# Gate and up products of an expert block in two 256-column halves, their inner rows formed and turned by halves

## The reference

```
for e in range(16):
    he = silu(t @ w_exp_gate[e]) * (t @ w_exp_up[e])          # 2048 -> 512
    out = out + gates[:, e:e+1] * (he @ w_exp_down[e])        # 512 -> 2048
```

## Time and profile before

| | |
|---|---|
| median of 3 runs | 1512.7 us (1511.94 to 1514.83) |
| profiled execution | 1513.4 us, its span 1511.6 us |
| mean granted TensorE clock | 0.973 |
| TensorE matmuls busy | 1381.8 us, 91% |
| weight loads / VectorE / ScalarE / GpSimd busy | 42% / 50% / 16% / 5% |
| DMA | 422.25 MB, mean 279 GB/s |
| expert stage: L976, first gate and up matmul | 992.5 us |
| expert stage: last down matmul ends, L1014 starts | 1483.8 us |

### The profile page before, as it was taken

How to read it: one execution, slowest core, us unless ns; L and a number is a source line. 1 busy time by engine, 2 the same in 40 slices (tenths; PEclk the granted TensorE clock), 3 DMA queues, 4 the chain that set the end, 5 groups by cost and what they waited for, 6 DMA issues and landing times.

```text
span 1511.6 us, 14234 instructions
## 1 busy us (share of the span) xinstructions
PE 1381.8 (91%) x5266; PEld 633.4 (42%) x5266; DVE 753.8 (50%) x1305; ACT 243.3 (16%) x409; POOL 75.5 (5%) x124
## 2 busy tenths in 40 slices
PE   4999999999998799999999999889898987898887
PEld 1435544444554455555544444533333332333332
DVE  1118799987767998989896612620000000000006
ACT  3101421000011111111122001511111111101104
POOL 2002000000010000000001000000000000000001
PEclk9999999999999899999999999989999999999989
DMA  9998656884677733331328634799999999999996
GB/s 356 409 373 261 230 184 227 272 266 147 198 252 267 246 109 105 104 118 64 113 82 311 221 111 167 284 380 426 428 406 414 427 427 427 427 396 426 426 411 274
DMA packets 138130, 422.25 MB, mean 279 GB/s; under 512 B 10230, under 2 KB 76033, under 8 KB 120949
## 3 DMA queue, kind: packets, MB, share of 16 engines
q1 hardware_dynamic: 124452, 375.85, 65.3%
q0 software_dynamic: 7520, 33.36, 6.1%
q10 hardware_dynamic: 6096, 12.20, 2.1%
HBM read 408.01 MB, written 22.58 MB: 285 GB/s over the span
## 4 chain that ended last, share of the span: by engine, by line
PE 68%; DMA 13%; DVE 12%; issue 3%; ACT 2%; SPq 0%; POOL 0%; DVEq 0%; ACTq 0%; POOLq 0%
PE ps L580 19%; PE ps L976 12%; PE ps L577 12%; DMA s_mem<-in_w_exp_gate 8%; PE ps L996 7%; DVE s_mem L1691 4%; DMA s_mem<-in_w_ada 4%; PE ps L497 3%; PE ps L858 3%; DVE s_mem L1895 2%; PE ps L755 1%; DVE s_mem L1866 1%; PE ps L439 1%; PE ps L706 1%; PE ps L454 1%
## 5 line engine op out<-in xcount | busy, mean ns | idle before, releaser
L1691 DVE SCALAR_TENSOR_TENSOR s_mem<-s_mem,s_sT 128x512 f32<-128x512 f32 x480 | 339.3, 748 | 32.9 <-DMA s_mem<-in_w_ada 16.1
L577 PE MATMUL ps<-s_mem 128*128 128x384 f32 x896 | 300.8, 491 | 0.0
L580 PE MATMUL ps<-s_mem 128*128 128x512 f32 x672 | 293.0, 594 | 0.7 <-ACT s_mem L1476 0.7
L976 PE MATMUL ps<-s_mem 128*64 128x512 f32 x1152 | 261.0, 610 | 18.4 <-DMA s_mem<-in_w_exp_gate 17.7
L577 PEld LDWEIGHTS ps<-s_mem 128*128 128x128 f32 x896 | 168.1, 191 | 124.9 <-issue 18.1
L580 PEld LDWEIGHTS ps<-s_mem 128*128 128x128 f32 x672 | 126.3, 190 | 158.3 <-issue 157.1
L976 PEld LDWEIGHTS ps<-s_mem 128*64 128x64 f32 x1152 | 88.0, 141 | 187.6 <-issue 186.7
L2197 DVE TENSOR_TENSOR s_mem<-s_mem,ps 64x512 f32<-64x512 f32 x18 | 12.2, 679 | 299.5 <-ACT s_mem L1568 299.5
L996 PE MATMUL ps<-s_mem 128*64 128x512 f32 x576 | 142.8, 654 | 9.3 <-DVE s_mem L2199 9.3
L996 PEld LDWEIGHTS ps<-s_mem 128*64 128x64 f32 x576 | 43.3, 148 | 95.4 <-issue 83.7
L2204 DVE COPY s_mem<-ps 128x512 f32<-128x512 f32 x18 | 12.4, 691 | 140.8 <-PE ps L996 140.8
(11 more groups left out here) (308 smaller groups left out, 1087.0 us busy)
## 6 DMA issues: line engine op xcount, KB each, us to landing
s_mem<-in_w_ada SPq DMA_DIRECT2D x256, 256.0 KB, 3.2
s_mem<-in_w_exp_gate SPq DMA_DIRECT2D x32, 2048.0 KB, 21.0
s_mem<-in_w_exp_up SPq DMA_DIRECT2D x32, 2048.0 KB, 24.9
s_mem<-in_w_exp_down SPq DMA_DIRECT2D x32, 2048.0 KB, 25.0
s_mem<-in_w_in SPq DMA_DIRECT2D x24, 2048.0 KB, 10.6
s_mem<-in_w_ada SPq DMA_DIRECT2D x16, 2048.0 KB, 16.6
s_mem<-in_w_out SPq DMA_DIRECT2D x8, 2048.0 KB, 9.7
y_slots<-s_mem ACTq DMA_DIRECT2D x34, 256.0 KB, 10.4
```

Of the source, the lines that this page charges most:

```text
L577: m = mm(ps[:, banks[m_], 0:TOK], v[:, k, m_ * P:(m_ + 1) * P], hT[:, kk, :], start=(kk == 0), stop=(kk == KT - 1))
L580: m = mm(ps[:, banks[m_], :], hT[:, kk, m_ * P:(m_ + 1) * P], v[:, k, :], start=(kk == 0), stop=(kk == KT - 1))
L976: m = mm(ps[half, 0, :], hgT[:, kh * 8 + k, :], weights(e, 2 * kh + which)[:, k, :], start=(kh + k == 0), stop=(kh * 8 + k == KT - 1), ski ...
L1691: v.op(ve.scalar_tensor_tensor(out=o, in0=w, scalar=scale, in1=o, op0=ALU.mult, op1=ALU.add), S("piece_used") if last else None)
```

## The change

Gate and up are computed in two halves of 256 columns. The loop over halves (nh) stands inside the loop over the two halves of the contraction (kh), so there are 128 matmuls of 256 columns in place of 64 of 512. A half doesn't take neighbouring columns: a view takes columns with index 0 and 1 modulo 4 for the first, 2 and 3 for the second, so that what the turns took with a step of four now lies contiguous in `he`. The first half stands in bank 0, the second in bank 7. A semaphore `first_half` is raised at the end of the first half. ScalarE and VectorE form `sg`, `he` and `heT` by halves. On TensorE the order after the products is: two turns for the first half (into bank 1), the row turns, a wait for the first turned half, the first of four down steps (4 matmuls each), two turns for the second half (into bank 0), the second step, a wait, the third and fourth. The down matmuls themselves stay as they are. Ahead of the first block TensorE waits until VectorE has read bank 7.

```diff
+        HALF_BANK = (0, 7)
...
             def expert_block(e, b):
-                pe.wait_ge(S("he_ready"), b + 1)
+                pe.wait_ge(S("he_ready"), b * 2 + 1)
                 pe.wait_ge(S("x_turned"), b * 2 + 2)
                 for kh in range(2):
                     for which in range(2):
                         weights_in(e, 2 * kh + which)
-                    for k in range(8):
-                        for which in range(2):
-                            half = slice(BLK * which, BLK * (which + 1))
-                            m = mm(ps[half, 0, :], hgT[:, kh * 8 + k, :], weights(e, 2 * kh + which)[:, k, :],
-                                   start=(kh + k == 0), stop=(kh * 8 + k == KT - 1), skip_group_check=True)
-                            if k == 7:
-                                m.then_inc(S(f"used{2 * kh + which}"), 1)
+                    for nh in range(2):
+                        for k in range(8):
+                            for which in range(2):
+                                half = slice(BLK * which, BLK * (which + 1))
+                                w = weights(e, 2 * kh + which)[:, k, :].rearrange("p (r q) -> p q r", q=4)
+                                out = ps[half, HALF_BANK[nh], 0:DE // 2].rearrange("p (q r) -> p q r", q=2)
+                                m = mm(out, hgT[:, kh * 8 + k, :], w[:, 2 * nh:2 * nh + 2, :], start=(kh + k == 0),
+                                       stop=(kh * 8 + k == KT - 1), skip_group_check=True)
+                                if k == 7 and nh == 1:
+                                    m.then_inc(S(f"used{2 * kh + which}"), 1)
+                                elif k == 7 and kh == 1 and which == 1:
+                                    m.then_inc(S("first_half"), 1)
+                def turn_hidden(h):
+                    pe.wait_ge(S("he_ready"), b * 2 + 2 + h)
+                    pe.nop(nofuse=True)
+                    for q in range(2):
+                        m = tr(ps[:, 1 - h, q * BLK:(q + 1) * BLK], he[:, (2 * h + q) * P:(2 * h + q + 1) * P],
+                               ident[0:BLK, 0:BLK])
+                    m.then_inc(S("he_turns"), 1)
+                def down_step(k):
+                    for n in range(4):
+                        half = slice(BLK * (n % 2), BLK * (n % 2 + 1))
+                        m = mm(ps[half, 4 + n // 2, :], heT[:, k, :], weights(e, 4 + k // 2)[:, k % 2, n * NCOL:(n + 1) * NCOL],
+                               start=(k == 0), stop=(k == 3), skip_group_check=True)
+                    if k % 2 == 1:
+                        m.then_inc(S(f"used{4 + k // 2}"), 1)
+                turn_hidden(0)
                 pe.wait_ge(S("x_gathered"), b * 16 + 16)
                 pe.nop(nofuse=True)
                 turn_rows()
-                pe.wait_ge(S("he_ready"), b + 2)
-                pe.nop(nofuse=True)
-                for q in range(4):
-                    m = tr(ps[:, 1, q * BLK:(q + 1) * BLK], he[:, q:DE:4], ident[0:BLK, 0:BLK])
-                m.then_inc(S("he_turns"), 1)
-                pe.wait_ge(S("he_turned"), b + 2)
+                pe.wait_ge(S("he_turned"), b * 2 + 2)
                 pe.wait_ge(S("y_read_act"), b + 1)
                 pe.wait_ge(S("y_read_dve"), b + 1)
...
+                weights_in(e, 4)
+                down_step(0)
+                turn_hidden(1)
+                down_step(1)
+                pe.wait_ge(S("he_turned"), b * 2 + 3)
+                weights_in(e, 5)
+                down_step(2)
+                down_step(3)
+
+            wait_read(pe, "dve", "index")
...
             def silu(b):
-                act.wait_ge(S("used3"), b + 2)
-                act.wait_ge(S("he_ready"), b + 1)
-                A(sg, ps[BLK:2 * BLK, 0, :], ACT.Silu).then_inc(S("sg_ready"), 1)
+                act.wait_ge(S("he_ready"), b * 2 + 1)
+                for h in range(2):
+                    act.wait_ge(*((S("first_half"), b + 1), (S("used3"), b + 2))[h])
+                    A(sg[:, h * DE // 2:(h + 1) * DE // 2], ps[BLK:2 * BLK, HALF_BANK[h], 0:DE // 2], ACT.Silu
+                      ).then_inc(S("sg_ready"), 1)
...
             def hidden(b):
-                dve.wait_ge(S("used3"), b + 2)
-                dve.wait_ge(S("sg_ready"), b + 1)
-                ve.tensor_tensor(he, sg, ps[0:BLK, 0, :], ALU.mult).then_inc(S("he_ready"), 1)
-                dve.wait_ge(S("he_turns"), b + 1)
-                ve.tensor_copy(heT.rearrange("p k s -> p (k s)"), ps[:, 1, 0:4 * BLK]).then_inc(S("he_turned"), 1)
+                for h in range(2):
+                    cols = slice(h * DE // 2, (h + 1) * DE // 2)
+                    dve.wait_ge(*((S("first_half"), b + 1), (S("used3"), b + 2))[h])
+                    dve.wait_ge(S("sg_ready"), b * 2 + 1 + h)
+                    ve.tensor_tensor(he[:, cols], sg[:, cols], ps[0:BLK, HALF_BANK[h], 0:DE // 2], ALU.mult
+                                     ).then_inc(S("he_ready"), 1)
+                    dve.wait_ge(S("he_turns"), b * 2 + 1 + h)
+                    ve.tensor_copy(heT[:, 2 * h:2 * h + 2, :].rearrange("p k s -> p (k s)"), ps[:, 1 - h, 0:2 * BLK]
+                                   ).then_inc(S("he_turned"), 1)
```

## The result

| | before | after |
|---|---|---|
| median | 1512.3 us (4 runs, 1511.90 to 1514.83) | 1701.4 us (4 runs, 1698.14 to 1702.34) |
| ratio after / before | | 1.123 [1.1211, 1.1249] |
| profiled execution, its span | 1513.4, 1511.6 | 1702.34, 1700.5 |
| mean granted TensorE clock | 0.973 | 0.987 |

The change makes the kernel 12.3% slower. The forecast was 1508.0 us, with a range up to 1513.5. The rival "strided reads at half rate", at 1679 us and a chance of 0.13, is what happened.

A forecast was written before the change was run, and what follows sets the result against it. The weights' arrival at 428 GB/s was taken to bound the expert stage, with TensorE costing 5.5 us in two holes. Closing all but 0.8 us gains 4.7 us, giving 1508.0 us, range 1505.0 to 1513.5.

The forecast's parts named there:

- strided reads at half rate: Gate and up take 27.6 us a block, a block 36.5, so TensorE sets the pace: 1679 us; chance 0.13.
- (b) Stride: Gate and up's moving operand read at every fourth float: priced at nothing; bounds nothing and half rate, 13.8 us a block.
- (a) Halves: Gate and up as 128 matmuls of 256 columns: 0.3 us a block taken, 0.6 at most, nothing at least.
- (c) The stop: TensorE's stop between gate/up and down: 2.0 us for 4.0, with table load, Silu and product off the path.
- (d) Waits and queues: Added waits and changed engine order cost nothing; the first block's bank wait, nothing to 0.3 us, taken as nothing.
- What bounds the kernel: Expert stage: weights' arrival at 428 GB/s, 31.8 us against TensorE's 26.6 a block; TensorE costs 5.5 us in two holes.
- The sum, 4.7 us: Two holes in the expert stage: 5.5 us lost, 0.8 left, the end following, hence 1508.0 us.
- hole: Dip in weight transfer at each expert with two blocks, as slot reloads wait for second block: 3.0 and 2.5 us.

The follow-up runs named there:

- layout alone: Kernel before with only the down matrix loaded as rows k*128 + p (8 KB runs) and `he` turned from contiguous columns: 1515.9 us, ratio 1.0025.
- change without stride: Changed kernel with halves of 256 neighbouring columns and the down matrix loaded as rows k*128 + p in 8 KB runs: 1514.0 us, ratio 1.0005.
- two neighbours: Changed kernel with halves taking columns {0, 1} and {2, 3} of every four, `he` turned in steps of two: 1512.2 us, ratio 0.9985.
- The two cut kernels: Kernel before and version reading two neighbours, each with half of every gate and up piece not loaded from the tenth load on: 1487.6 and 1450.9 us.

## Why the forecast was wrong

One block's gate and up, 64 pairs of 512 columns or 128 matmuls in pairs of 256, by how the moving operand is read. All are pieces of chains at the full granted clock:

| kernel | read | us a block |
|---|---|---|
| before, and layout alone | contiguous | 13.78 |
| change without stride | contiguous, halves | 13.81 |
| stride 8 bytes | 2 of each 16 bytes | 14.55 |
| two neighbours | 2 of each 16 bytes, halves | 14.50 |
| **changed kernel** | 1 of each 16 bytes, halves | 28.87 |
| stride 16 bytes | 1 of each 16 bytes | 28.85 |
| stride 32 bytes | 1 of each 32 bytes | 29.43 |

**(b) Stride: the step that failed**, "I take nothing, since the row has that rate per element with a wider stride". The price is 28.87 - 13.81 = 15.1 us a block, above the upper bound of 13.8. It makes a block 37.7 us, above the 31.8 that the transfers need, so that TensorE sets the pace and every block pays. The forecast had weighed the Trainium skill's rule ("Advanced Engine Details and Errata", SBUF Cachelines: lines of 16 bytes, at least two hits on one to keep the rate) against L915's load and let the load win. The table bears the rule out in the main on the moving side: two hits a line cost 5%, where the rule would have them free, one hit doubles the time, and a wider step adds 2%.

What was wrong was the comparison, not the row. L915's strided load (194 ns) was set against the moving side's pace per column. The like of it is another turn's load, and the trace of before had them, in the list of groups:

```profile
L915 PEld LDWEIGHTS ps<-s_base,s_mem 128*128 128x128 f32 x152 | 18.4, 194 | 16.2 <-issue 16.2
...
L883 PEld LDWEIGHTS ps<-s_base,s_mem 128*128 128x128 f32 x48 | 5.2, 142 | 1.6 <-ACT s_mem L1537 1.4
...
L797 PEld LDWEIGHTS ps<-s_base,s_mem 128*128 128x128 f32 x48 | 5.0, 140 | 6.3 <-ACT s_mem L1476 5.1 <-issue 0.9 <-DVE s_mem L1658 0.3
```

L797 and L883 turn contiguous columns in 140 and 142 ns. The step was in plain sight as 54 ns, and the run with contiguous turns made 140 of the 194. Nor does the stationary side scale to the moving one: 39% there, 109% here. Bounded by half rate the sum was open from 1508 to 1679 us, and the value was taken at one end of it on a row of the other side of the array.

**(a) Halves: right.** 13.81 against 13.78, 0.03 us for the 0.3 taken.

**(c) The stop: right in kind, cheaper.** 1.63 us (1.85 with turns that step by two) for the 2.0. One part didn't go as said: the table load does not come in the last quarter but at the block's start, at 1187.43. Before, it came after the wait for `used3`. In the code the wait that stands directly ahead of the Silu was `he_ready` and is now `first_half` or `used3`; I take it that the load goes ahead of the last wait. That order alone was not tried.

**(d) Waits and queues: right.** No wait for the added semaphores stands in the chain.

**What bounds the kernel: right.** The two cut kernels and the 53.0 and 44.1 us of waiting for weights show it. It is also why a stop that is 2 us shorter in 18 blocks gives 2.3 us in all.

**The sum, 4.7 us: of the right kind, too large.** It belongs to a change that costs no stride; two neighbours to a read is the nearest. The load that opens a hole should be issued 2.5 us before the one ahead lands. Measured are 1135.6 against 1138.2, 2.6 before, so the first hole is closed; and 1331.0 against 1331.7, 0.7 before, so 1.8 us of the second stay, where 0.4 was forecast. That is 3.7 us by the queue, and 2.3 (0.4 to 4.2) by the run times. The second falls short in the stretch from the gate load's landing to the issue: it began with a half block that took 9.06 us after a wait, against 7.47 in the first hole, and took 25.4 us in all where 24.8 were charged.

**The rival's own size.** It took the pairs at exactly half rate (27.6 us) and the stop at 2.0, hence 36.5 us a block and 1679. Measured are 28.87 and 1.63, 37.66 a block. 18 x 1.16 = 21 us of the 22 between 1679 and 1701.

## What to carry to other kernels

Read a moving operand so that at least two neighbouring floats of every 16 bytes come together; where a later step wants columns interleaved, give each half pairs of neighbours and put the remaining step into the small stationary loads. Price an access pattern by rows of the same side of the array and the same shape that differ in the pattern alone, and where no such row exists let neither end of the bounds be the value. Where the weights' arrival sets the pace, a shorter stop on TensorE is worth only the holes that it closes (2.3 us here, 36.7 without that limit).

## What was not expected of the hardware

- The stationary load pays a step already at 8 bytes: 64x128 loads in the turns of `he` take 137 ns contiguous, 203 at every second float, 209 at every fourth. The moving side pays 5% at 8 bytes and 109% at 16. Little of it reaches TensorE's path: in the timeline the eight row turns take 1.16 us strided and 1.09 contiguous.

Turns of `he` in the layout alone (contiguous) and with two neighbours (every second float):

```profile
L986 PEld LDWEIGHTS ps<-s_base,s_mem 64*128 64x128 f32 x72 | 5.8, 137 | 33.8 <-issue 33.8
```
```profile
L992 PEld LDWEIGHTS ps<-s_base,s_mem 64*128 64x128 f32 x72 | 11.2, 203 | 21.9 <-issue 21.9
```

- The two matmuls of a pair in the column halves read their operands at rates of their own: 1.08 us beside 0.6 in one pair, and the pair costs the slower one's 0.91.
- Weight runs of 8 KB in place of 16 KB, for a third of the bytes, cost 0.25% [0.09, 0.41] of the kernel. (The turns of `he` are contiguous in that run too.)
